# ACT and DVE part heavy units further ahead of PE in the expert stretch: MOE_LEAD from 3 to 5

## What is computed

```python
logits = (hf @ router).astype(jnp.float32)
top_val, top_idx = lax.top_k(logits, TOP_K)
gates = jax.nn.softmax(top_val, axis=-1)
...
# for each expert e, on the tokens that chose it:
(jax.nn.silu(h @ wg[e]) * (h @ wu[e])) @ wd[e]
...
# each token gets the sum of its two experts' rows, times their gates
```

## Time and profile before

| what | value |
|---|---|
| median of 3 runs | 1429.22 us |
| the profiled execution's own time | 1428.27 us |
| its span, first to last instruction | 1426.5 us |
| PE busy, share of the span | 1387.9 us, 97% |
| DVE busy | 854.5 us, 60% |
| ACT busy | 697.4 us, 49% |
| HBM read | 440.61 MB |
| expert loads | 384 of 896 KB, issued from 533.15 to 1370.07 us |

### The profile page before, as it was taken

One profiled execution on the slowest core, in us unless ns is written; L12 is line 12 of the kernel. 1 busy time (PEld: TensorE's weight loads), 2 busy tenths in 40 slices (PEclk: granted clock), 3 DMA queues, 4 the chain that ended last, 5 costly groups with the idle time before them and its releaser, 6 DMA issues.

```text
span 1426.5 us, 18333 instructions
## 1 busy us (share of the span) xinstructions
PE 1387.9 (97%) x7015; PEld 1004.9 (70%) x7015; DVE 854.5 (60%) x988; ACT 697.4 (49%) x785; POOL 6.9 (0%) x14
## 2 busy tenths in 40 slices
PE   6999999999999999999999999999999999999997
PEld 6877888888887788766666666666666766666635
DVE  6997636463479978746454656455555455555426
ACT  6566534442555657544444444444444453544316
POOL 0000000000000000000000000000000000000000
PEclk9999999999999999999999999999999999999998
DMA  9425565555544009999999999999999999999992
GB/s 334 158 66 172 178 191 190 180 182 201 167 150 146 8 5 417 421 419 419 420 413 420 419 418 420 414 416 419 418 419 419 415 415 419 418 420 419 419 410 92
DMA packets 99670, 443.89 MB, mean 311 GB/s; under 512 B 7729, under 2 KB 22097, under 8 KB 99329
## 3 DMA queue, kind: packets, MB, share of 16 engines
q1 hardware_dynamic: 98688, 439.30, 78.5%
q0 software_dynamic: 896, 3.44, 0.7%
HBM read 440.61 MB, written 2.10 MB: 310 GB/s over the span
## 4 chain that ended last, share of the span: by engine, by line
PE 84%; DMA 6%; DVE 6%; ACT 2%; issue 1%; ACTq 0%; DVEq 0%; SPq 0%
PE psum L642 19%; PE psum L643 18%; PE psum L644 18%; PE psum L1176 11%; PE psum L1190 7%; DMA ring<-in_moe_w_up 4%; DMA ring<-in_moe_w_down 2%; PE psum L693 2%; PE psum L1080 1%; PE psum L711 1%; ACT w_hi L1506 1%; PE psum L1205 1%; DVE arena_a L2105 1%; DVE ring_lo L2018 1%; PE psum L665 1%
## 5 line engine op out<-in xcount | busy, mean ns | idle before, releaser
L2018 DVE TENSOR_TENSOR ring_lo<-ring,w_hi 128x1792 fp32r<-128x1792 f32 x191 | 384.3, 2023 | 278.8 <-ACT w_hi L1506 277.3
L1506 ACT ACTIVATE w_hi<-ring 128x1792 fp32r<-128x1792 f32 x191 | 323.8, 1700 | 286.4 <-DMA ring<-in_moe_w_down 119.0
L644 PE MATMUL psum<-w_hi,hidden_b 128*128 128x512 f32 x624 | 229.6, 368 | 0.0
L2012 DVE TENSOR_TENSOR ring_lo<-ring,w_hi 128x2048 fp32r<-128x2048 f32 (+1 forms) x68 | 152.6, 2265 | 101.4 <-ACT w_hi L1500 101.4
L1176 PE MATMUL psum<-ring,xT 128*64 128x512 f32 (+1 forms) x1024 | 201.7, 543 | 0.0
L642 PE MATMUL psum<-w_hi,hidden_b 128*128 128x512 f32 (+1 forms) x512 | 190.3, 372 | 1.9 <-DVE ring_lo L2018 1.8
L643 PE MATMUL psum<-ring_lo,hidden_b 128*128 128x512 f32 (+1 forms) x512 | 187.1, 365 | 0.0
L642 PE MATMUL psum<-w_hi,xT_parts 128*128 128x512 f32 (+1 forms) x384 | 150.0, 391 | 1.9 <-DVE ring_lo L2012 1.8
L1176 PEld LDWEIGHTS psum<-ring,xT 128*64 128x64 f32 x1024 | 69.8, 137 | 114.1 <-issue 112.0
L642 PE MATMUL psum<-w_hi,hidden_a 128*128 128x512 f32 (+1 forms) x384 | 146.7, 382 | 2.7 <-DVE ring_lo L2018 2.7
L644 PE MATMUL psum<-w_hi,xT_parts 128*128 128x512 f32 (+1 forms) x384 | 148.6, 387 | 0.0
(11 more groups left out here) (338 smaller groups left out, 1453.8 us busy)
## 6 DMA issues: line engine op xcount, KB each, us to landing
ring<-in_moe_w_gate SPq DMA_DIRECT2D x128, 896.0 KB, 8.9
ring<-in_moe_w_up SPq DMA_DIRECT2D x128, 896.0 KB, 9.8
ring<-in_moe_w_down SPq DMA_DIRECT2D x128, 896.0 KB, 9.5
ring<-in_w_in SPq DMA_DIRECT2D x16, 1024.0 KB, 6.0
ring<-in_dense_w_gate SPq DMA_DIRECT2D x14, 1024.0 KB, 5.1
ring<-in_dense_w_up SPq DMA_DIRECT2D x14, 1024.0 KB, 5.1
ring<-in_dense_w_down SPq DMA_DIRECT2D x14, 1024.0 KB, 4.9
ring<-in_w_out SPq DMA_DIRECT2D x8, 1024.0 KB, 5.1
```

The source lines that it names most:

```text
L644: return mm(o, a[1], b[0], start=False, stop=final)
L1506: A(heavy_high(c), moe_raw(m), ACT.Copy).then_inc(hi_ready, 1)
L2012: V.tensor_tensor(low(g, sizes[g]), raw(g, sizes[g]), f32(high(g, sizes[g])), ALU.subtract).then_inc(lo_ready, 1)
L2018: V.tensor_tensor(moe_low(m), moe_raw(m), f32(heavy_high(c)), ALU.subtract).then_inc(lo_ready, 1)
```

## The change

`MOE_LEAD` becomes 5, and the parting of the first units, which stand ahead of the loop over the places, covers the units 2, 3 and 4 in place of 2 alone. `LEAD`, of the dense layer, stays.

```diff
-LEAD, MOE_LEAD = 3, 3
+LEAD, MOE_LEAD = 3, 5
...
                     first_light()
-                    moe_split(0, 2, 2)
+                    for c in range(2, MOE_LEAD):
+                        moe_split(0, c, c)
...
                 first_heavy(1)
-                moe_split(0, 2, 2)
+                for c in range(2, MOE_LEAD):
+                    moe_split(0, c, c)
```

## The result

The changed kernel takes 1470.39 us (median of 4 runs, 1466.78 to 1472.15) against 1428.45 before (4 runs): a ratio of 1.0285, with a 95% interval of 1.0271 to 1.0298. It is slower by 41.9 us. 1459 with a range of 1440 to 1474 was forecast. The profiled execution took 1469.88 us, its span 1468.1, which is 41.6 more than before.

The account below looks back on a forecast made before the run. The prediction took the weight stream and PE (97% busy) as both tight. Waits beyond the stream's reserve, 29.7 us for pairs 1 to 3, plus 1.7 for pair 0, minus 1.3 at the end, gave 30.1 us: 1459 us, range 1440 to 1474.

Parts of the forecast that it names:

- the four kinds: Tasks at a block's third light place: `add_back` 0, `add_back` 2, first two light `add_back`, `light_hi`; together 9.9 us a pair.
- Item 1: `add_back` 0 behind L9 comes after the third parting: PE waits 4.0 us, 3.7 after the stream's reserve.
- Item 2: `add_back` 2 behind L13 comes after `gated` and more partings: PE waits 4.9 us, 2.5 after the reserve.
- Item 3: The two light `add_back` behind L25 come after the third parting: PE waits 4.3 us more, 3.5 after the reserve.
- Item 4: `light_hi` behind L33 comes after ACT's third parting: PE waits 2.0 us, 0.2 after the reserve.
- the tasks at the first light place: `silu`, `gated`, `take_heavy_y` now behind the first unit's parting: costed at nothing, at most 2.02 us each if cover is gone.
- the start of the stretch: First 20 heavy units in a row, units 3 and 4 parted ahead: between -2.02 and +2.02 us, taken as 0.
- The floor of 6.4 us: Shortest load time from issue to landing before the stream loses time; PE's lateness above that reserve costs time.
- rows 4: Profile rows of the dense layer, where loads hardly queue: 1024 KB land after 5.1 us, bounding the floor from below.
- The queue covers it all: Rival: waiting loads keep the stream full and PE makes its lateness good, 1429 to 1432 us; chance 0.06.
- the absorbed half: Rival: the floor lies near 4 to 5 us, so slower but little, 1437 to 1447 us; chance 0.2.
- Faster: Rival: first units of a block parted without tasks ahead, so PE's waits for parted units shrink, 1423 us; chance 0.04.

Follow-up runs that it names:

- ACT at 5: The changed kernel with a lead of 5 on ACT only and DVE back at 3: 1441.57 us, ratio 1.0087 to the kernel before.

## Why the prediction was right, and where its sum was off

**The mechanism was right.** ACT's waits are for landings (121.5 us for the down matrix, 119.0 before, and still 0.48 us between two partings), so the longer lead gained nothing, and the tasks at the third light place fell behind three partings. Moving only the tasks of the four kinds back took 25 us away, `gated` and `silu` with them 38, and the remaining adds too 39. The time, 1470.39 us, lies near the upper end of the range.

**The items, in pair 1, were near.** PE's own waits, from its timeline:

```profile
746.28 0.55 PE L1213 MATMUL psum<-par,xT 128*128 128x128 f32 x3 [0.77 <-ACT xT L1824]
...
783.40 0.50 PE L1087 MATMUL psum<-hidden_b 128*128 128x512 f32 x1 [2.53 <-DVE h L2536]
...
802.66 0.50 PE L1087 MATMUL psum<-hidden_b 128*128 128x512 f32 x1 [1.04 <-DVE h L2536]
...
897.21 0.55 PE L1213 MATMUL psum<-par,xT 128*128 128x128 f32 x3 [1.34 <-ACT xT L1824]
```

Item 1, with the wait behind L3 that it was said to cover, was put at 3.7 us; PE waited 0.77 + 2.53 = 3.3. Item 2 was put at 2.5; PE waited 1.04. Item 3 at 3.5 us more than before; PE waited 5.31 against 1.09, so 4.2 more. Item 4 at 0.2; PE waited 1.34. Together 9.9 us forecast, 9.9 measured. Items 2 and 4 missed by over a microsecond each and in opposite directions, so part of that agreement is luck.

**What failed** is the completeness of the sum: 30.1 us against 41.6 in the profiled execution. What is missing is the clock, which no term had, and the tasks at the first light place, which were put at nothing.

```profile
722.75 0.50 PE L642 MATMUL psum<-w_hi,hidden_b 128*128 128x512 f32 x1
...
934.29 0.50 PE L642 MATMUL psum<-w_hi,hidden_b 128*128 128x512 f32 x1
```
```profile
727.83 0.50 PE L642 MATMUL psum<-w_hi,hidden_b 128*128 128x512 f32 x1
...
951.83 0.50 PE L642 MATMUL psum<-w_hi,hidden_b 128*128 128x512 f32 x1
```

These are the starts of H0 of pairs 1 and 2, before and after. PE is 5.1 us late at the first and 17.5 at the second. Pairs 2 and 3 cost 13.1 and 13.8 us more, and at H44 PE gets 1.4 back, as forecast (1.3).

1. *The clock*, in no term. Pair 1 cost 12.5 us in place of 9.9; 2.3 of the difference are the scatter behind L27 and H28 at half speed. Four stretches at 0.50 stand in the trace, and keeping PE busy in one wait a pair gave 5.2 us back. Half of PE's busy time in the four (18.9 us) is an estimate of their whole cost, 9.5 us; with the 31.5 us of new waits that makes 41.0 of the 41.6.
2. *Pair 0*, 5.1 us in place of 1.7. The step "the start of the stretch" took 0 within one parting, because PE would wait for the stream later anyway. PE waited 2.7 us for `gated` behind H19's parting, and was still 2.7 us late at H28 (635.44 for 632.75). The other 2.4 us come at H32 and H33, from `gated` again. The term that the sum had for pair 0, `light_hi` behind L33, did not come: PE was late by then and has no such wait there.
3. *The tasks at the first light place were costed at nothing.* The step said that four light units cover them. They cover most of PE's wait for the task, but not the second parting, which the task now delays. Moved alone in the kernel before, `gated` cost 7.1 us, and putting it and `silu` back took 13 us off the kernel whose four kinds were back already. In the changed kernel itself it is seen in pair 0, where DVE and PE stand like this:

```profile
652.75 2.08 DVE L2515 TENSOR_TENSOR arena_b<-psum,arena_b 128x896 f32<-128x896 f32 x2
...
655.71 3.96 DVE L2019 TENSOR_TENSOR ring_lo<-ring,w_hi 128x1792 fp32r<-128x1792 f32 x2
```
```profile
653.94 0.47 PE L642 MATMUL psum<-w_hi,hidden_a 128*128 128x512 f32 x1 [2.38 <-issue]
...
657.79 0.39 PE L642 MATMUL psum<-w_hi,hidden_a 128*128 128x256 f32 x1 [0.88 <-DVE ring_lo L2019]
```

H32 needs the bank that the first half of `gated` frees, and H33 the second parting. Before, PE waited 1.36 us ahead of H32 and not at H33. In pairs 1 to 3 neither wait is seen, since PE is late there by then for other reasons.

**The floor of 6.4 us is a slope, not an edge.** In the changed kernel the first block of pair 1, 5 us later than before, got 351 GB/s with loads landing 6.0 us after issue, and a load issued with none ahead of it landed after 4.6, not 4.2 as one expectation above has it (windows, then DMA issues of 714 to 722.5 us and of 864 to 866 us):

```profile
714.00:727.00 13.00, 13.00 (x68) 8.36 (x68) 5.03 (x5) 5.33 (x5) 0.00 (x0) 1.00 0.99 351
```
```profile
ring<-in_moe_w_gate SPq DMA_DIRECT2D x4, 896.0 KB, 6.0
...
ring<-in_moe_w_down SPq DMA_DIRECT2D x1, 896.0 KB, 4.6
```

So the rate falls from 420 GB/s to 402 at 6.7 us and to 351 at 6.0: the sign that loads would land nowhere far under 6.4 us at the full rate held. What the queue does is make a later wait for a landing shorter, as the sum had it; it doesn't take up PE's lateness itself (10.9 of 11.6 us came out). One reading beside it was off: the 5.1 us of rows 4 lies 0.7 us above the formula that the prediction quotes (4.4 us for 1024 KB), not half a microsecond; no term hangs on it.

**The rivals.** "The queue covers it all" and "the absorbed half" fell with the time, 41.9 us over the kernel before, and the first of them with that run too. "Faster" fell with the adds, which came late in every pair from 1 on. The claim that the longer lead would not let ACT part sooner was right.

## What to carry to other kernels

When a queue that works strictly in order holds both prefetch work, which waits for transfers, and small tasks, which another engine waits for, a longer lead moves the small tasks behind transfers that have yet to land. Look at what the prefetch waits for: if it is the landing, more lead gains nothing, and each task's place has to be moved along with it. Count also the work that a moved task pushes back, not only who waits for the task.

## What the runs showed of the hardware that was not expected

- While PE stood still for 5.31 us, the granted clock fell to 0.50, the 1.2 GHz level, and stayed there for 6.8 us. The wait and the slow work behind it together cost some 7.6 us (5.31 + 2.3). Matmuls whose result nobody reads, in unused columns of a bank, kept it at 1.00.
- The length of a wait alone did not settle whether the clock fell. Behind waits of 3.11 us (the changed kernel), 2.37 and 2.01 (ACT at 5) and 1.87 (`gated` moved alone) it was at 0.50 for 3.4 us; behind waits of 2.53 and 2.54 us in the changed kernel it stayed at 1.00.
- A 896 KB load into an empty queue landed after 4.6 us. The stream ran at 420 GB/s with loads landing after 8.8 us, at 402 with 6.7, and at 351 with 6.0.
- 3.1 us taken off PE's waits changed the time by nothing that can be measured, and 11.6 us of lateness added to PE came out as 10.9. Where PE and the stream are both this near to binding, the time is blind to a small gain on one of them and open to every loss.
